# Second block of a two-block model: products on operands that are not yet normed

## What is computed

```python
def rmsnorm_2(x, g):
    y = xf * lax.rsqrt(jnp.mean(xf * xf, axis=-1, keepdims=True) + RMS_EPS)
    return (y * g.astype(jnp.float32)).astype(x.dtype)

def retention_mixer(hn, w_in, gn_g, w_o, cos, sin, valid):
    proj = hn @ w_in                       # q, k (rotated), v, gate
    ...
    return (jax.nn.silu(gate) * on.astype(dt)) @ w_o

def swiglu(hn, w1, w3, w2):
    return (jax.nn.silu(hn @ w1) * (hn @ w3)) @ w2

def second_block(x, meta, ...):
    ...
    for layer in range(DEPTH_2):
        hn = rmsnorm_2(h, norm_mix_g[layer])
        if layer < N_A_LAYERS:
            h = h + retention_mixer(hn, ret_w_in[layer], ...)
        else:
            kv_a = rmsnorm_2(h, norm_kv_g) @ w_kv_a      # in mla_shared_kv
            c_kv = rmsnorm_2(kv_a[..., :MLA_KV_RANK], kv_a_norm_g)
            cq = rmsnorm_2(hn @ w_q_a, q_a_norm_g)       # in mla_mixer
            ...
        h = h + swiglu(rmsnorm_2(h, norm_ffn_g[layer]), ffn_w1[layer], ...)
    return rmsnorm_2(h, final_g)[:, PAD + N_META:]
```

## Time and profile before

| | us |
|---|---|
| median of 3 runs | 1800.28 (1798.26 to 1801.43) |
| profiled run | 1799.95 |
| its span | 1798.0 |
| TensorE busy | 1549.2 |
| VectorE busy | 736.7 |
| ScalarE busy | 582.3 |
| Pool busy | 178.9 |
| expert loop, by the page's slices | about 390 to 850 |

### The profile page before, as it was taken

How to read it: one execution, slowest core, us unless ns; L and a number is a source line. 1 busy time by engine, 2 the same in 40 slices (tenths; PEclk the granted TensorE clock), 3 DMA queues, 4 the chain that set the end, 5 groups by cost and what they waited for, 6 DMA issues and landing times.

```text
span 1798.0 us, 28287 instructions
## 1 busy us (share of the span) xinstructions
PE 1549.2 (86%) x12178; PEld 1276.6 (71%) x12178; DVE 736.7 (41%) x1201; ACT 582.3 (32%) x865; POOL 178.9 (10%) x119
## 2 busy tenths in 40 slices
PE   6999799888676767767599999989998899989997
PEld 5998546864343434444498976989998876679997
DVE  4355854352121111111572446354445453355543
ACT  5347543211010111111433432344433443344432
POOL 2000000100000000000100001034411210024410
PEclk8999899969888989888799999999999999799999
...
GB/s 278 143 140 78 1 94 1 3 308 418 429 428 429 428 430 428 430 428 346 188 182 150 141 169 1 106 134 183 144 163 180 118 89 94 94 100 187 153 165 52
DMA packets 31987, 360.91 MB, mean 201 GB/s; under 512 B 5280, under 2 KB 8224, under 8 KB 9632
## 3 DMA queue, kind: packets, MB, share of 16 engines
...
## 4 chain that ended last, share of the span: by engine, by line
PE 65%; DMA 18%; DVE 7%; ACT 4%; issue 2%; POOL 1%; SPq 1%; ACTq 0%; DVEq 0%; PEld 0%
PE PS L462 38%; DMA expert_w<-in_w 18%; PE PS L475 5%; PE PS L824 3%; PE PS L511 3%; PE PS L492 2%; PE PS L844 2%; PE PS L940 2%; PE PS L667 2%; ACT wh L1155 1%; DVE wl L1591 1%; DVE rs L1622 1%; SPq L337 1%; PE PS L677 1%; POOL UL L2135 1%
## 5 line engine op out<-in xcount | busy, mean ns | idle before, releaser
L1591 DVE TENSOR_TENSOR wl<-raw,wh 128x4096 fp32r<-128x4096 f32 (+2 forms) x74 | 303.5, 4101 | 290.7 <-ACT wh L1155 290.6
L462 PE MATMUL PS<-UH,wh 128*128 128x272 f32 (+1 forms) x1160 | 336.9, 290 | 15.0 <-DVE wl L1647 9.6
L462 PE MATMUL PS<-UL,wh 128*128 128x272 f32 (+1 forms) x1160 | 334.0, 288 | 0.0
L462 PE MATMUL PS<-UH,wl 128*128 128x272 f32 (+1 forms) x1160 | 334.0, 288 | 0.0
L1155 ACT ACTIVATE wh<-raw 128x4096 fp32r<-128x4096 f32 (+2 forms) x75 | 252.0, 3360 | 179.9 <-PE PS L462 163.3
L824 PE MATMUL PS<-expert_w,XW 128*32 128x256 f32 x2048 | 163.3, 474 | 104.3 <-DMA expert_w<-in_w 104.3
L462 PEld LDWEIGHTS PS<-UH,wh 128*128 128x128 f32 x1160 | 220.2, 190 | 17.3 <-DVE wl L1647 10.0
L462 PEld LDWEIGHTS PS<-UL,wh 128*128 128x128 f32 x1160 | 220.8, 190 | 0.5
L462 PEld LDWEIGHTS PS<-UH,wl 128*128 128x128 f32 x1160 | 220.8, 190 | 0.0
L824 PEld LDWEIGHTS PS<-expert_w,XW 128*32 128x32 f32 x2048 | 74.7, 131 | 181.7 <-issue 91.3
L1939 DVE TENSOR_TENSOR SG<-PS,SG 128x128 f32<-128x128 f32 x32 | 9.3, 291 | 299.6 <-ACT SG L1356 299.6
(11 more groups left out here) (408 smaller groups left out, 2698.1 us busy)
## 6 DMA issues: line engine op xcount, KB each, us to landing
...
raw<-in_ret_qk SPq DMA_DIRECT2D x4, 2048.0 KB, 11.0
...
```

Source lines behind the costliest of these rows:

```text
L462: mm = pe.matmul(gbank(g)[:, c0:T], w[:, c:c + P], x(k)[:, c0:], start=(k == 0 and j == 0), stop=(k == nk - 1 and j == 2))
L1591: dve.tensor_tensor(WL[n % 2][:, 0:w], RAW[n % 3][:, 0:w], WH[n % 2][:, 0:w].bitcast(F32), ALU.subtract).then_inc(lo_done, 1)
```

## The change

Products in the second block take operands that carry the gain but not the token's scale. When a block of H is complete, ScalarE squares it into one of two ring tiles (`ring_square`) and rounds H·gain to UH (`scaled`), VectorE makes UL = H·gain − UH (`remainder`), and the Pool adds the squares up (`accumulate`); TensorE sums over partitions once per norm (`total`), in the midst of the next group of units. The scale is applied where a product is read: folded into the tables for rotated q and k, as a scale per token column of ScalarE's read-out for v (`scale_columns` makes that column), by a multiplication on VectorE elsewhere. In up, FT = bank·scale, then the sigmoid of FT, then FT·sigmoid, FU as before. down adds bank·scale to H in two instructions. The read-outs of kvc, krq, qar, kn, qr and qn move to VectorE. `norm_step` between the units goes.

At the end of the experts, the additions to H, the remainders and the quarters of the first slab's lower half alternate on VectorE; the first block's final norm is folded in, by G2 and GFG, made on the Pool earlier. The first slab of ret_qk has a tile of its own (RAWX, where the second WL stands) and is loaded behind the first two experts, which are loaded earlier too. In the head loop, quarters are rounded one step earlier at the start, and `lo_part` comes one step later.

```diff
-MLA_PIECES = {0: (("kv_b", 2),), 1: (("kv_b", 3),), 2: (("q_b", 0),), 3: (("q_b", 1),),
-              4: (("q_b", 2), ("q_b", 3)), 10: (("mla_o", 0),), 11: (("mla_o", 1),), 12: (("mla_o", 2),),
+MLA_PIECES = {0: (("kv_b", 3),), 1: (("q_b", 0),), 2: (("q_b", 1),), 3: (("q_b", 2), ("q_b", 3)), 10: (("mla_o", 0),), 11: (("mla_o", 1),), 12: (("mla_o", 2),),
...
+            sp.wait_ge(lo_done, N_FIRST)
+            expert(0, 0)
+            load(XPT[2][:], a["w2"][0], xp_full[2])
+
+            sp.wait_ge(freed["dve"], FREED[UNIT0["wo"] + 7][1])
+            expert(1, 1)
+            load(XPT[5][:], a["w2"][1], xp_full[5])
+            slab(N_FIRST)
...
+                    before(k)
+                    if parts is not None:
+                        pe.wait_ge(nhi_done, parts[0] + k + 1)
+                        pe.wait_ge(nlo_done, parts[1] + k + 1)
...
+            def total(count, acc, bank, c0=0):
+
+                pe.wait_ge(acc_done, count)
+                pe.matmul(bank[:, c0:T], ones[:], acc[:, c0:], start=True, stop=True).then_inc(ssq_done, 1)
...
-            for m in range(KB):
-                norm_step(UMT, m, KB)
-            pe.wait_ge(var_done, 3)
-            norm_sum(SQ3, KB)
-
-            n = FIRST_SLAB["ret_qk"]
-            for h in range(RH):
+            pe.wait_ge(msq_done, 1)
+            pe.wait_ge(sq_done, 17)
+            def both_norms(k):
+
+                pe.wait_ge(sq_done, 16 + k + 1)
+                mm = pe.matmul(sbank(0)[:, META:T], G2[:, k, :], SQ3[:, k, META:], start=(k == 0), stop=(k == KB - 1))
+                if k == KB - 1:
+                    mm.then_inc(ssq_done, 1)
...
                 n = FIRST_SLAB[f"up{layer}"]
                 for s in range(11):
                     slab_ready(n + s)
                     if s == 0:
-                        products_as_normed(UNIT0[f"up{layer}"], 4, n, KB, *U, parts, c0)
+                        products_as_split(UNIT0[f"up{layer}"], 4, n, KB, *x, parts, c0,
+                                          lambda k: total(squares, NACC, sbank(0), c0) if k == 4 else None)
...
-                    if s:
-                        norm_step(sq_next, s - 1, KB, c0)
...
+            products_as_split(UNIT0["kn"], 4, n, 4, *CK, None, 0,
+                              lambda k: pe.wait_ge(freed["dve"], FREED[UNIT0["kvc"] + k][1]))
+            total(34, ACCQ, sbank(2), META)
+            scale_columns(5)
...
+                c = GAINS[gain] + k
+                act.activation(dst, src, ACT.Copy, scale=gains[:, c:c + 1]).then_inc(nhi_done, 1)
...
+                if j >= 2:
+                    act.wait_ge(acc_done, 8 + j - 1)
+                act.activation(NSQ[:, j % 2, c0:], src, ACT.Square).then_inc(sq_done, 1)
...
             for m in range(KB):
                 act.wait_ge(moe_out, m + 1)
-                squares(UMT[:, m, :], H[:, m, :])
+                act.activation(UH[:, m, META:], H[:, m, META:], ACT.Copy, scale=GFG[:, m:m + 1]).then_inc(nhi_done, 1)
+                act.activation(SQ3[:, m, META:], H[:, m, META:], ACT.Square).then_inc(sq_done, 1)
+                if m < 3:
+                    hi_part(N_FIRST, m + 1)
             std()
...
-            std()
-            for k in range(KB):
-                high(UH[:, k, :], SQ3[:, k, :], 24 + k + 1)
             hi(N_FIRST + 1)
...
+                    act.wait_ge(freed["dve"], FREED[UNIT0["gate"] + j][1])
                     if j == 0:
                         act.wait_ge(rqk_done, 8)
                     if j >= 2:
-                        act.wait_ge(freed["dve"], FREED[g - 2][1])
-                    act.activation(GSIG[j % 2][:], gbank(g)[:, 0:T], ACT.Sigmoid).then_inc(gsig_done, 1)
+                        act.wait_ge(gate_t, j - 1)
+                    act.activation(GSIG[j % 2][:], GATE[:, j, :], ACT.Sigmoid).then_inc(gsig_done, 1)
...
                 hi(n + 1)
+                std(c0=c0)
...
+                    act.wait_ge(freed["dve"], FREED[UNIT0[f"up{layer}"] + 2 * p][1])
+                    act.activation(FS[p % 2][:, c0:], FT[p % 2][:, c0:], ACT.Sigmoid).then_inc(f_sig, 1)
...
+            hi(FIRST_SLAB["kv_c"] + 1)
             std()
-            for k in range(KB):
...
+                act.wait_ge(unit_done, g + 1)
+                ring_square(gbank(g)[:, c], c.start)
+                scaled(hi_tile[:, k, c], gbank(g)[:, c], gain, k)
...
+            def remainder(dst, src, high, gain, k):
+
+                c = GAINS[gain] + k
+                return dve.scalar_tensor_tensor(out=dst, in0=src, scalar=gains[:, c:c + 1], in1=high.bitcast(F32),
+                                                op0=ALU.mult, op1=ALU.subtract)
...
             for m in range(8):
                 dve.tensor_tensor(H[:, m, META:], gbank(m // 2)[:, SEQ * (m % 2):SEQ * (m % 2) + SEQ],
                                   H[:, m, META:], ALU.add).then_inc(moe_out, 1)
+                if m:
+                    split_of_sum(m - 1)
+                if m < 4:
+                    lo_part(N_FIRST, m)
+            split_of_sum(7)
             dve.wait_ge(moe_out, 8)
             freeing(dve.nop(), 4)
-            lo(N_FIRST)
+            norms[0] += 1
+            dve.wait_ge(ssq_done, norms[0])
+            dve.tensor_scalar(rs[:, 0:META], sbank(1)[:, 0:META], 1.0 / D, EPS, ALU.mult, ALU.add)
+            dve.tensor_scalar(rs[:, META:], sbank(0)[:, META:T], 1.0 / D, EPS * EPS, ALU.mult, ALU.add)\
+                .then_inc(var_done, 1)
+            root(rs)
+            dve.wait_ge(tab2_in, 48)
+            dve.tensor_tensor(cosw[:], cosw[:], rs[:], ALU.mult)
+            link(dve.tensor_tensor(sinw[:], sinw[:], rs[:], ALU.mult))
             lo(N_FIRST + 1)
...
                 lo(n + 1)
+                scale_of(D, c0=c0)
                 f0 = FB * layer
                 for p in range(FB):
                     g = UNIT0[f"up{layer}"] + 2 * p
+                    ft, fu = FT[p % 2][:, c0:], FU[p % 2][:, c0:]
+                    dve.wait_ge(unit_done, g + 1)
+                    freeing(dve.tensor_tensor(ft, gbank(g)[:, c0:T], rs[:, c0:], ALU.mult))
                     dve.wait_ge(f_sig, f0 + p + 1)
-                    freeing(dve.tensor_tensor(FT[p % 2][:, c0:], gbank(g)[:, c0:T], FS[p % 2][:, c0:], ALU.mult))
-                    dve.wait_ge(freed["dve"], FREED[g][1])
+                    link(dve.tensor_tensor(ft, ft, FS[p % 2][:, c0:], ALU.mult))
                     dve.wait_ge(unit_done, g + 2)
                     if p >= 2:
                         dve.wait_ge(f_lo, f0 + p - 1)
-                    freeing(dve.tensor_tensor(FU[p % 2][:, c0:], gbank(g + 1)[:, c0:T], FT[p % 2][:, c0:], ALU.mult))
+                    freeing(dve.tensor_tensor(fu, gbank(g + 1)[:, c0:T], ft, ALU.mult))
                     if p % 2 and n + p // 2 + 2 < len(SLABS):
                         lo(n + p // 2 + 2)
+            def scaled_sum(layer, s, c0=0):
+
+                g = UNIT0[f"down{layer}"] + s
+                dve.wait_ge(unit_done, g + 1)
+                freeing(dve.tensor_tensor(FT[s % 2][:, c0:], gbank(g)[:, c0:T], rs[:, c0:], ALU.mult))
+                dve.wait_ge(freed["dve"], FREED[g][1])
+                dve.tensor_tensor(H[:, s, c0:], FT[s % 2][:, c0:], H[:, s, c0:], ALU.add).then_inc(h_new, 1)
...
+            for k in range(KB):
+                dve.wait_ge(nhi_done, 32 + k + 1)
+                remainder(U2L[:, k, late], H[:, k, late], U2H[:, k, late], "mix1", k).then_inc(nlo_done, 1)
             n = FIRST_SLAB["kv_c"]
             lo(n + 1)
-            normed(SQQ, H, "mix1", KB, META)
+            scale_of(D)
+
+            def latent(g, k, high, low, gain, c, count):
+
+                dve.wait_ge(nhi_done, count)
+                freeing(remainder(low[:, k, c], gbank(g)[:, c], high[:, k, c], gain, k))
+
+            for u in range(4):
+                latent(UNIT0["kvc"] + u, u, CKH, CKL, "kva", slice(0, T), 40 + u + 1)
+            dve.wait_ge(unit_done, UNIT0["krq"] + 1)
+            freeing(dve.tensor_tensor(KR2[:], gbank(UNIT0["krq"])[:, 0:T], rs[:], ALU.mult))
             lo(n + 2)
-            scale_of(4 * P, lambda: lo(FIRST_SLAB["kv_a"]))
-            normed(SQQ, CKRAW, "kva", 4)
+            for u in range(3):
+                latent(UNIT0["krq"] + 1 + u, u, CQH, CQL, "qa", late, 44 + u + 1)
+            lo(FIRST_SLAB["kv_a"])
+            dve.wait_ge(freed["dve"], FREED[UNIT0["krq"]][1])
+            scale_of(4 * P, bank=1, eps=EPS * EPS)
+            for u in range(3):
+                latent(UNIT0["qar"] + u, 3 + u, CQH, CQL, "qa", late, 47 + u + 1)
             lo(FIRST_SLAB["q_r"])
-            scale_of(6 * P, c0=META)
-            normed(SQQ, CRAW, "qa", 6, META)
-            dve.wait_ge(mla_in, 32)
...
+                freeing(dve.tensor_tensor(dst, gbank(g)[:, c], t[:, c], ALU.mult))
+
+            for u in range(4):
+                scaled_out(UNIT0["kn"] + u, KN[:, u, :], rs, slice(0, T))
+            scale_of(6 * P, RQS, 2, EPS * EPS, META)
```

(14 more changed lines are left out.)

487 lines of the change are left out of this document (296 added, 191 removed).

## The result

| | before | changed |
|---|---|---|
| median, us | 1799.27 (1797.76 to 1801.43, 4 runs) | 1757.59 (1755.44 to 1759.73, 4 runs) |
| ratio, 95% interval | | 0.974 (0.969 to 0.979) |
| profiled run, span | 1799.95, 1798.0 | 1756.81, 1755.0 |

41.7 us faster, where 51 were forecast: inside the range of 1738 to 1765, and 9 us above the forecast of 1749. A second set of runs of the changed kernel gave 1755.09 (1751.8 to 1757.85), so medians of four executions of one program can differ by 2.5 us. The kernel before ranged over 4 us in this call and over up to 22 us in later ones.

The account below looks back on a forecast made before the run. TensorE, busy 86% of the span, was taken as the bound, so gains lay where it stops or does norm work. Terms summed to 51.7 us: 1799.95 − 51.7 + 0.3 = 1748.6, say 1749 us; range 1738 to 1765.

Parts of the forecast that it names:

- The signs: Expected in the changed profile: second ret_qk slab about 890, retention to up0 under 1 us, no lower-quarter or up-slab stops.
- E: Start of the latent-attention layer, down0's end to first scores: 89.5 us becomes 77.9, gain 11.5, with two stops.
- A: End of the experts to the second slab's products: 10 us less, minus a second cold start of 2, gain 7.5.
- D: down0: six norm steps of 0.46 us between products fall away, gain 2.7 us.
- H: down1: six norm steps of 0.43 us fall away, gain 2.5 us.
- C: Retention's output product and hand-over to up0: norm steps, hand-over wait and a shorter first slab, gain 11.0 us.
- G: mo and hand-over, head loop's end to the end of up1's first slab: 50.5 us becomes 37.6, gain 13.
- The early expert loads: First two experts' loads issued earlier: costed at 0, at most 1 us gained.
- Rival 1: Up slabs become bound by the VectorE–ScalarE chain, beside the Pool: 12 us, giving 1761; chance 12%.
- a cold start of about 2 us at three stops: TensorE slower after pauses: 2 us at each of ret_qk's first two slabs, 1.8 at krq.
- Term B: Retention: three tiny matmuls for the column scale, 0.3, and one more multiply ending the gates, 0.5; loss 0.8 us.
- Term F: Latent head loop, 86.2 us: moved quarters remove the 2.5 and most of the 3.8 us stops; gain 5, bounds 0 and 8.

Follow-up runs that it names:

- experiment 2: Changed kernel with the latents' remainders on VectorE ahead of root and reciprocal at the start of the latent-attention layer: 1746.55 us.
- experiment 3: Changed kernel with the second slab of ret_qk rounded and subtracted ahead of root and reciprocal: 1752.67 us.
- experiment 8: Changed kernel with two ones-products put back on TensorE after each of 30 units, as in the old norm steps: 1767.01 us.
- experiment 7: Changed kernel with two more VectorE instructions in each of the 22 gate and value pairs of both feed-forwards: 1765.15 us.
- experiment 4: Changed kernel with VectorE weighing retention's first head's scores ahead of the last gate's three multiplications: 1752.05 us.
- experiment 5: Kernel before with two multiplications by 1.0 added ahead of weighing retention's first scores: 1803.5 us, ratio 1.000 to before.
- experiment 9: Changed kernel with the output matrix's quarters in other steps of the head loop, subtracted in steps 11, 13 and 15: 1749.30 us.
- experiment 1: Changed kernel and kernel before run again, nothing edited: 1755.09 us and 1800.88 us.

## Why the prediction was right, and where it was off

**What held.** Sign and place, and in the first profile the size: each term of the second block is within 1.7 us of the table. The signs came too: the second slab at 892 us, 0.8 us from the last retention product to up0, no stop at a lower quarter in the head loop, no stop in the up slabs. The stops of E were put at 3.4 and 4.5 us and measured 2.8 and 4.5, released by the remainders CKL and CQL as said; experiment 2 shows that their place behind root and reciprocal was the cause. In A the second slab starts 36.6 us behind the sum, forecast 37.1; the queue behind the root is confirmed by experiment 3. D and H, steps at their own length, are borne out by experiment 8. The largest gains, the two hand-overs to the feed-forwards with their first slabs in C and G, are read off the rows of the two traces alone; no run put a hand-over back. The early expert loads, costed at 0, gave nothing that stands out.

**Rival 1** did not come: no stop in 22 up slabs. The slack of 0.53 us is thin, as experiment 7 shows; two more instructions a pair cross it. The contention that was to bring it about does not meet the change's own multiplication, which takes 0.43 us as alone, since the Pool's remainder starts after it; it does meet an instruction that follows at once, 0.92 us in place of 0.42 in experiment 7.

**The step that failed: costs of the clock.** The sum took a cold start of about 2 us at three stops, two in A and one in E, and nothing else. Four things came out otherwise. (a) Term B: the gates' last stop was priced at 0.5 us, its own growth, 2.04 to 2.68 us (it grew by 0.64), with nothing for what follows it. In five of eight profiles of kernels with this stop the heads of retention then ran 5 to 8 us longer. If the profiles stand for all executions this is the largest loss, an estimated 4 us on the mean (five in eight of some 7). That the stop itself brings it about is not shown: experiment 4 goes that way, experiment 5 does not. (b) Term F: 5 forecast, 3.4 measured. 2.9 us of stops remained at the two turns, forecast 1.7, with the granted clock at 0.50 behind them, and experiment 9, which shortens them, gave 5.6 us. (c) Term G, 13 against 11.7. The 2.2 us of stops inside mo are gone; mo's eight units take 25.5 us in one row of products, where 8 by 2.85 are 22.8, as the loop's low clock reaches into them:

```profile
1527.80:1532.80 5.00, 5.00 (x24) 4.95 (x24) 4.80 (x3) 0.12 (x1) 0.00 (x0) 0.50 0.16 69
```

The kernel before shows it too, 7.80 us for mo's first 48 matmuls, which the sum took at 2.85 for 24. The hand-over, a stop of 1.3 us and the total's 0.4, was put at 1.2 for both. (d) In this profile the first block lost 4.1 us at half clock, which no term could hold; experiment 1 shows that it comes and goes between executions.

**Terms mis-sized.** C, 11.0 against 9.8: five steps, not six, stood between the products of the last three slabs (2.1 in place of 2.7), the hand-over gave 5.8 in place of 6.2 and the slab 1.8 in place of 2.1. A, 7.5 against 6.9: the second slab starts 10.5 us sooner, but 3.6 of them go again before ret_v, 0.75 of these in the column scale's small matmuls, which B had at 0.3.

What stays open: what decides whether, and for how long, the clock is low behind a stop of 2 to 5 us, at the gates, at krq and at kn.
